# Two-layer attention and FFN block in one kernel: the residual add after each norm moved from VectorE to GpSimd

## The chip, the cores and the metric

One NeuronCore of one Trainium2 chip runs the whole program. The metric is the device time of one execution in microseconds, as the median of three runs. All times below are microseconds unless marked otherwise.

## The reference

Two decoder layers over 256 tokens and 2048 features, everything in float32. Layer 0 has sliding-window attention with sinks, layer 1 a compressed, selected and windowed attention; both have a convolutional feed-forward part with 5632 hidden features. What matters here is how a layer is joined up: each of its two parts works on a normalised copy of `x`, and its result is normalised again before it is added to `x`.

```python
def rmsnorm(x, g):
    xf = x.astype(F32)
    y = xf * lax.rsqrt(jnp.mean(xf * xf, axis=-1, keepdims=True) + RMS_EPS)
    return (y * g.astype(F32)).astype(x.dtype)

def reference(x, norm_g, ...):
    for i in range(DEPTH):
        g = norm_g[i]
        h = rmsnorm(x, g[0])
        ...
        x = x + rmsnorm(mix, g[1])
        h = rmsnorm(x, g[2])
        x = x + rmsnorm(conv_ffn(h, ffn_w_gate[i], ffn_w_up[i], ffn_conv_w[i], ffn_conv_b[i], ffn_w_down[i]), g[3])
    return x
```

## The kernel before

The weights come in as 703 chunks of 128 x 1024 through a ring of four buffers (`raw`). ScalarE copies each chunk to a rounded high part (`whi`, line 1268), VectorE subtracts to get the low part (`wlo`, line 1713, called a split below), and TensorE multiplies high and low parts with the high and low parts of the activations (`hs`). All orders are written out by hand: each engine has one program, and semaphores join them.

`x` lies in SBUF with tokens on the partitions, as `x_sb[128, 8 chunks, 2 token tiles, 256 features]`; `y`, the result of a layer's part, has the same form. `y` is made by units of 512 features (two chunks); the last of them (k = 3) ends in two PSUM banks, one for each token tile, and is multiplied there by the norm's gains (`gain_rows`). The factor r of y's norm is one number per token, `r_token[:, t]`, ready for token tile 0 first (`inverse_of_y`, line 1770).

There are four places where `y` times r is added to `x`. Three of them are followed by the next norm and the next matmuls (called norm A after layer 0's attention, norm B between the layers, norm C after layer 1's attention); the fourth is the end of the program, the tail. In norms A, B and C VectorE runs `norms`: it adds the first 128 features of chunk 0, token tile by token tile (line 1934), then the rest of chunk 0, scales y's last token tile (`last_y`), and then adds the chunks 1 to 7 in between its other work (`add_y`, line 1901): the low parts of the new `hs` (`low_of_h`, line 1787) and the splits of the weights g0+3 to g0+7. TensorE turns each chunk of `x` by four transposes (`turn_x`, line 852) into PSUM, one chunk ahead of the one that it multiplies: before chunk c of the first unit it turns chunk c+1, waits for `h_ready` of chunk c, and then does 16 products and their low parts. ScalarE (`prenorm`) makes the high part of chunk c (`high_of_h`, line 1338), then the weight copy of chunk c+2 of the following ones, then the squares of x for the next norm's sum:

```python
for c in range(CH):
    high_of_h(n, gain, c)
    if 1 <= c <= 5:
        split(g0 + c + RING - 2)
    if 2 <= c <= 5:
        square_x(n, c - 2)
```

`square_x(n, q)` squares the chunks 2q and 2q+1 and waits until they are added. So the squares of the chunks 6 and 7 (q = 3) stand in ScalarE's queue behind chunk 5's high part and ahead of chunk 6's.

In the tail TensorE sums chunks 0 and 1 itself, by products with the identity and with a diagonal of r; VectorE adds the chunks 2 to 7 (lines 1923 and 1901), TensorE turns them, ScalarE copies them to `out_f` (line 1701), and SyncE sends them off in six transfers.

GpSimd works in the attention (lines 640 to 674), copies 128 x 16 coefficients per feed-forward unit (line 691), and makes layer 1's bias tables (lines 552 to 594), which start just when norm B does.

## Time and profile before

| what | value |
|---|---|
| time, median of 3 runs | 2131.49 (2131.29 to 2131.70) |
| span of the profiled execution | 2130.6 |
| TensorE busy | 2115.8 (99%) |
| VectorE, ScalarE, GpSimd busy | 63%, 50%, 12% |
| norm C: last product of the unit before to first product of the next | 1370.46 to 1373.33 |
| tail: last product with weights starts, span ends | 2117.16, 2130.6 |

A row of the timeline gives start, duration, engine, line and operation, and in brackets how long the engine stood idle before it and what ended that. Rows that follow each other are merged with a count (x4), and their duration is then that of all. Durations on GpSimd are rough, so the spacing of its rows counts as much.

### The profile page before, as it was taken

The page shows a single profiled execution, that of the slowest core. Times are in us where ns is not written, and L with a number is a line of the kernel's source. Part 1 is how long each engine was busy: PE and PEld are TensorE (multiplying, and loading weights), DVE is VectorE, ACT ScalarE, POOL GpSimd, SP SyncE. Part 2 cuts the span into 40 slices and gives each one's busy share as a digit, 9 for nine tenths or more (in the row PEclk, how much of TensorE's full clock was granted, in tenths as well). Part 3 has the DMA queues.
Part 4 walks back from the last instruction along what each step waited for, and adds up shares of the span by engine and source line. Part 5 has one row for each costly group of instructions (what it writes and reads, how often), then busy time and mean ns, then how long its engine had stood idle before and what let it go on. Part 6 is the DMA issues. An engine that isn't in the chain of part 4 may idle for free.

```text
span 2130.6 us, 34642 instructions
## 1 busy us (share of the span) xinstructions
PE 2115.8 (99%) x12227; PEld 1811.8 (85%) x12227; DVE 1334.2 (63%) x2031; ACT 1065.4 (50%) x1620; POOL 259.4 (12%) x411
## 2 busy tenths in 40 slices
PE   9999999999999999999999999999999999999998
PEld 8997788888888888888999977888888888888887
DVE  7665676766767754445866654676766767754443
ACT  6675554444444444444656776554444444444443
POOL 4452000000000000002204662000000000000000
PEclk9999999999999999999999999999999999999999
DMA  7444555555555565554673233455555565565553
GB/s 252 144 166 152 175 177 196 180 192 183 179 203 179 189 213 189 188 188 161 222 234 119 100 110 128 166 177 194 182 190 186 178 200 184 187 212 188 188 188 124
DMA packets 107504, 381.42 MB, mean 179 GB/s; under 512 B 14146, under 2 KB 14866, under 8 KB 106770
## 3 DMA queue, kind: packets, MB, share of 16 engines
q1 hardware_dynamic: 105106, 373.63, 52.1%
q10 hardware_dynamic: 2304, 6.53, 0.8%
q8 instruction: 61, 1.00, 0.2%
q14 instruction: 33, 0.27, 0.0%
HBM read 377.97 MB, written 2.14 MB: 178 GB/s over the span
## 4 chain that ended last, share of the span: by engine, by line
PE 96%; DVE 2%; ACT 0%; issue 0%; DMA 0%; SPq 0%; DVEq 0%; ACTq 0%
PE set L708 32%; PE set L801 31%; PE set L712 16%; PE set L926 10%; PE set L1000 2%; PE set L974 1%; PE set L1029 1%; PE set L852 1%; PE set L976 0%; PE set L1031 0%; DVE block_f L2133 0%; DVE wlo L1713 0%; DVE x_sb L1901 0%; DMA raw<-in_stream 0%; PE set L1098 0%
## 5 line engine op out<-in xcount | busy, mean ns | idle before, releaser
L1713 DVE TENSOR_TENSOR wlo<-raw,whi 128x1024 fp32r<-128x1024 f32 x703 | 860.9, 1235 | 578.8 <-ACT whi L1268 575.5
L1268 ACT ACTIVATE whi<-raw 128x1024 fp32r<-128x1024 f32 x703 | 738.2, 1058 | 732.8 <-PE set L712 350.2
L708 PE MATMUL set<-hs,whi 128*128 128x512 f32 x2932 | 966.3, 395 | 0.8 <-ACT whi L1268 0.8
L712 PE MATMUL set<-hs,wlo 128*128 128x256 f32 x2944 | 695.6, 281 | 0.0
L712 PEld LDWEIGHTS set<-hs,wlo 128*128 128x128 f32 x2944 | 544.7, 188 | 61.0 <-DVE wlo L1713 0.4
L708 PEld LDWEIGHTS set<-hs,whi 128*128 128x128 f32 x2932 | 503.3, 189 | 71.0 <-DVE hs L1803 1.0
L801 PE MATMUL set<-whi,hid 128*128 128x512 f32 x1408 | 388.3, 395 | 0.0
L801 PEld LDWEIGHTS set<-whi,hid 128*128 128x128 f32 x1408 | 264.1, 188 | 65.7 <-DVE wlo L1713 0.6
L801 PE MATMUL set<-wlo,hid 128*128 128x512 f32 x704 | 224.1, 395 | 0.0
L926 PE MATMUL set<-hs,whi 128*128 128x256 f32 x1280 | 213.1, 286 | 1.7 <-DVE v_raw L2163 1.4
L926 PEld LDWEIGHTS set<-hs,whi 128*128 128x128 f32 x1280 | 176.2, 189 | 5.0 <-DVE v_raw L2163 1.8
L801 PEld LDWEIGHTS set<-wlo,hid 128*128 128x128 f32 x704 | 132.2, 188 | 31.0
L801 PE MATMUL set<-whi,os 128*128 128x512 f32 x512 | 147.6, 398 | 0.0
L691 POOL COPY cw<-conv_sb 128x16 f32 x20 | 40.8, 2040 | 854.0 <-DVE gate L2272 854.0
L926 PE MATMUL set<-hs,wlo 128*128 128x256 f32 x640 | 131.9, 281 | 0.0
L801 PEld LDWEIGHTS set<-whi,os 128*128 128x128 f32 x512 | 94.5, 188 | 20.1
L1740 DVE TENSOR_TENSOR gate_in<-half,set 128x256 f32<-128x256 f32 x176 | 62.3, 417 | 67.7 <-ACT half L1280 67.7
L926 PEld LDWEIGHTS set<-hs,wlo 128*128 128x128 f32 x640 | 99.9, 188 | 0.0
L1472 ACT ACTIVATE probs<-scored,neg_max 128x128 f32<-128x128 f32 x192 | 85.5, 450 | 14.8 <-DVE neg_max L2007 14.8
L650 POOL TENSOR_SCALAR probs<-probs,recip,gates 128x128 f32<-128x128 f32 (+1 forms) x128 | 84.8, 675 | 66.2 <-DVE recip L2041 66.2
L801 PE MATMUL set<-wlo,os 128*128 128x512 f32 x256 | 89.8, 405 | 0.0
L1280 ACT ACTIVATE half<-set 128x1024 f32<-128x1024 f32 x46 | 47.2, 1026 | 80.7 <-PE set L708 80.7
(209 smaller groups left out, 1339.9 us busy)
## 6 DMA issues: line engine op xcount, KB each, us to landing
raw<-in_stream SPq DMA_DIRECT2D x703, 512.0 KB, 3.4
gain_rows<-rows ACTq DMA_DIRECT2D x4, 1024.0 KB, 4.7
xT<-in_x SPq DMA_DIRECT2D x8, 256.0 KB, 8.2
out_y<-out_f SPq DMA_DIRECT2D x3, 512.0 KB, 3.6
bo_rows<-rows ACTq DMA_DIRECT2D x1, 1024.0 KB, 7.2
wg_raw<-in_w_gates ACTq DMA_DIRECT2D x1, 768.0 KB, 5.1
raw<-in_stream SPq DMA_DIRECT2D x2, 256.0 KB, 3.9
w2k_sb<-in_w ACTq DMA_DIRECT2D x2, 128.0 KB, 8.0
```

Of the source, the lines that this page charges most:

```text
L650: ins = nc.gpsimd.tensor_scalar(e, e, r, gates[:, t, c:c + 1], ALU.mult, ALU.mult)
L691: nc.gpsimd.tensor_copy(cw[:].rearrange("p a b -> p (a b)"), conv_sb[:, layer, f, :]).then_inc(cw_ready, 1)
L708: return mm(sets[set_of(u)][:, t, 0:2 * w], whi[:, slot, cols], r, start=first, stop=final)
L712: return mm(sets[set_of(u)][:, t, w:2 * w], wlo[:, slot, cols], r[:, 0:w], start=False, stop=False)
L801: ins = mm(sets[0][:, CK * (k % 2) + t, :], source[:, kt, part], w[:, g % RING, cols], start=kt == 0 and i == 0, stop=final)
L926: ins = mm(sets[0][:, banks[t // 2], (t % 2) * S:(t % 2 + 1) * S], w, r[:, S:2 * S] if i == 1 else r[:, 0:S], start=kt == 0 and i == 0 and ...
L1000: ins = nc.tensor.transpose(ps_turned[:, t * P:(t + 1) * P], e[:, t * P:(t + 1) * P], ident[:])
L1268: A(whi[:, slot, :], raw[:, slot, :], ACT.Copy).then_inc(hi_ready, 1)
L1280: A(half[:, st, :, 0:width], sets[st][:, :, 0:width], ACT.Copy).then_inc(half_ready, UT)
L1472: ins = A(probs[:, pair_block % 2, b, h, cols], scored[:, b, h, cols], ACT.Exp, bias=neg_max[:, b, h, t:t + 1], scale=-1.0, accum_out=sums ...
L1713: V.tensor_tensor(wlo[:, slot, :], raw[:, slot, :], whi[:, slot, :].bitcast(F32), ALU.subtract).then_inc(lo_ready, 1)
L1740: ins = V.tensor_tensor(dst(t), h, b, ALU.add)
```

## The change

GpSimd gets a new piece of program, `add_residual`. In norms A, B and C it does all of the chunks 1 to 7: for each, two multiplications by r (one for each token tile), a wait for them, and one addition of 128 x 512. Between chunks 1 and 2 it scales y's last token tile by the gains. Since GpSimd can't read PSUM, ScalarE copies that tile from PSUM to `y` first (`copy_last_y`, in norms B and C between the two token tiles of the first high part; after layer 0's attention it lies in SBUF already). VectorE keeps chunk 0, the low parts and the splits. TensorE and the squares wait for the new semaphore `x_more`. In the tail GpSimd adds chunk 4 and then scales the last tile; VectorE adds the chunks 2, 3, 5 and token tile 0 of 6 and 7, waits for `y_last`, adds token tile 1 of 6 and 7, and then copies chunk 7 from PSUM to `out_f` in ScalarE's place. TensorE's own sums in the tail now go chunk by chunk.

```diff
+TAIL_ADDED = ((2, 3, 5, 6, 7), (4,))
...
+            def scale_last_y(n):
+                gain = gain_rows[:, 3 * UNIT:4 * UNIT].rearrange("p (a f) -> p a f", a=CK)
+                part = y[:, 3 * CK:4 * CK, 1, :]
+                pool.wait_ge(rows_in, 16 * (n + 1))
+                pool.wait_ge(y_squared, 8 * n + 8)
+                pool.wait_ge(evacuated, UT * ((O0, DN0, O1, DN1)[n] + 4))
+                nc.gpsimd.tensor_tensor(part, part, gain, ALU.mult).then_inc(y_last, 1)
+                pool.wait_ge(y_last, n + 1)
+
+            def add_residual(n, parts):
+                if n == 0:
+                    pool.wait_ge(y_scaled, 7)
+                else:
+                    pool.wait_ge(evacuated, UT * ((DN0, O1, DN1)[n - 1] + 3) + CK)
+                for k, c in enumerate(parts):
+                    if n < 3 and c == 2:
+                        scale_last_y(n)
+                    for t in range(TT):
+                        pool.wait_ge(y_inverse, TT * n + t + 1)
+                        nc.gpsimd.tensor_scalar(y[:, c, t, :], y[:, c, t, :], r_token[:, t:t + 1], 1.0, ALU.mult,
+                                                ALU.mult).then_inc(y_times_r, 1)
+                    pool.wait_ge(y_times_r, TT * ((CH - 1) * n + k + 1))
+                    nc.gpsimd.tensor_tensor(x_sb[:, c], x_sb[:, c], y[:, c], ALU.add).then_inc(x_more, 1)
+                if n == 3:
+                    scale_last_y(n)
...
@@ turn_x (TensorE)
-                    pe.wait_ge(x_ready, CH * (n - 1) + c + 1 - (TURNED_SUMS if n == 4 else 0))
+                elif n < 4:
+                    pe.wait_ge(x_more, (CH - 1) * (n - 1) + c)
...
@@ square_x (ScalarE)
-                    act.wait_ge(x_ready, CH * (n - 1) + CK * (q + 1))
+                    act.wait_ge(x_ready, n)
+                    act.wait_ge(x_more, (CH - 1) * (n - 1) + CK * q + 1)
...
+            def copy_last_y(n):
+                act.wait_ge(evacuated, UT * ((DN0, O1, DN1)[n - 1] + 3) + CK)
+                A(y[:, 3 * CK:4 * CK, 1, :], sets[0][:, CK + 1, :].rearrange("p (a f) -> p a f", a=CK),
+                  ACT.Copy).then_inc(evacuated, CK)
...
@@ norms (VectorE)
                 add_y(0, 1, x_ready, 1, slice(P, FC))
-                last_y()
                 low_of_h(n + 1, gain, 0)
-                add_y(1, 2, x_ready, 1)
-                add_y(2, 4, x_ready, 2)
                 low_of_h(n + 1, gain, 1)
                 split(g0 + 3)
                 low_of_h(n + 1, gain, 2)
-                add_y(4, 6, x_ready, 2)
                 split(g0 + 4)
                 low_of_h(n + 1, gain, 3)
-                add_y(6, 8, x_ready, 2)
                 split(g0 + 5)
...
@@ tail (VectorE)
-                    for c in range(3, CH):
+                    for c in (3, 5):
                         add_y(c, c + 1, x_ready, 1)
-                        if c == 4:
-                            last_y()
+                    for t in range(TT):
+                        if t == 1:
+                            dve.wait_ge(y_last, n + 1)
+                        for c in (6, 7):
+                            ins = V.scalar_tensor_tensor(x_sb[:, c, t, :], y[:, c, t, :], r_token[:, t:t + 1], x_sb[:, c, t, :],
+                                                         ALU.mult, ALU.add)
+                            if t == 1:
+                                ins.then_inc(x_ready, 1)
+                    dve.wait_ge(x_turned, CH * 5)
+                    for kt in range(CK):
+                        V.tensor_copy(out_f[:, KT - CK + kt, :],
+                                      norm_banks[4][:, (CH - 1) % UT, kt * S:(kt + 1) * S]).then_inc(out_more, 1)
```

VectorE's queue at norm A, before (`hs` is the activations' high and low part, `wlo` a split):

```order
L1770 RECIPROCAL r_token<-root 128x1
L1934 SCALAR_TENSOR_TENSOR x_sb<-y,r_token,x_sb 128x128
L1901 SCALAR_TENSOR_TENSOR x_sb<-y,r_token,x_sb 128x128 x2
L1873 TENSOR_TENSOR y<-y,gain_rows 128x2x256
L1784 SCALAR_TENSOR_TENSOR hs<-set,g_sb,hs 128x128 x2
L1787 SCALAR_TENSOR_TENSOR hs<-set,g_sb,hs 128x256
L1901 SCALAR_TENSOR_TENSOR x_sb<-y,r_token,x_sb 128x256 x2
L1901 SCALAR_TENSOR_TENSOR x_sb<-y,r_token,x_sb 128x2x256 x2
L1787 SCALAR_TENSOR_TENSOR hs<-set,g_sb,hs 128x256 x2
L1713 TENSOR_TENSOR wlo<-raw,whi 128x1024
```

and now:

```order
L1815 RECIPROCAL r_token<-root 128x1
L1982 SCALAR_TENSOR_TENSOR x_sb<-y,r_token,x_sb 128x128
L1946 SCALAR_TENSOR_TENSOR x_sb<-y,r_token,x_sb 128x128 x2
L1829 SCALAR_TENSOR_TENSOR hs<-set,g_sb,hs 128x128 x2
L1832 SCALAR_TENSOR_TENSOR hs<-set,g_sb,hs 128x256 x3
L1758 TENSOR_TENSOR wlo<-raw,whi 128x1024
```

All adds behind chunk 0 and the last scaling are gone from this queue; the low parts and the splits have closed up. GpSimd's queue at the same place, with what its instructions wait for (the copy of `cw` was the next instruction there before, and now stands behind all of these):

```order
L635 TENSOR_SCALAR y<-y,r_token 128x256 [waits y_inverse,y_scaled]
L635 TENSOR_SCALAR y<-y,r_token 128x256 [waits y_inverse]
L638 TENSOR_TENSOR x_sb<-x_sb,y 128x512 [waits y_times_r]
L621 TENSOR_TENSOR y<-y,gain_rows 128x2x256 [waits evacuated,y_squared,rows_in]
L635 TENSOR_SCALAR y<-y,r_token 128x256 [waits y_inverse,y_last]
L635 TENSOR_SCALAR y<-y,r_token 128x256 [waits y_inverse]
L638 TENSOR_TENSOR x_sb<-x_sb,y 128x512 [waits y_times_r]
L635 TENSOR_SCALAR y<-y,r_token 128x256 [waits y_inverse] x2
L638 TENSOR_TENSOR x_sb<-x_sb,y 128x512 [waits y_times_r]
```

The last two rows come for each chunk from 3 to 7. What VectorE did in 8 instructions behind chunk 0's, GpSimd does in 22, one behind the other.

## Rows read from the trace of the kernel before

**Rows 1.** The page: span, busy time of TensorE, the chain that ended last.

```profile
span 2130.6 us, 34642 instructions
...
PE 96%; DVE 2%; ACT 0%; issue 0%; DMA 0%; SPq 0%; DVEq 0%; ACTq 0%
```

**Rows 2.** The timeline of TensorE in norm C and at norm A's start.

```profile
1375.49 0.66 PE L852 MATMUL set<-ident,x_sb 128*128 128x128 f32 x4 [0.44 <-DVE x_sb L1901]
1377.38 0.60 PE L852 MATMUL set<-ident,x_sb 128*128 128x128 f32 x4
1377.99 0.73 PE L708 MATMUL set<-hs,whi 128*128 128x512 f32 x2
...
1390.60 0.60 PE L852 MATMUL set<-ident,x_sb 128*128 128x128 f32 x4
...
1393.83 0.60 PE L852 MATMUL set<-ident,x_sb 128*128 128x128 f32 x4
1394.18 0.72 PE L708 MATMUL set<-hs,whi 128*128 128x512 f32 x2
...
252.82 0.33 PE L852 MATMUL set<-ident,x_sb 128*128 128x128 f32 x1 [1.49 <-DVE x_sb L1934]
```

**Rows 3.** The timeline of VectorE and ScalarE in norm C.

```profile
1371.93 0.16 DVE L1770 RECIPROCAL r_token<-root 128x1 f32<-128x1 f32 x1 [0.28 <-ACT root L1428]
...
1372.40 0.61 DVE L1901 SCALAR_TENSOR_TENSOR x_sb<-y,r_token,x_sb 128x128 f32<-128x128 f32 x2
...
1383.19 1.41 DVE L1901 SCALAR_TENSOR_TENSOR x_sb<-y,r_token,x_sb 128x512 f32<-128x512 f32 x2
...
1389.68 0.62 ACT L1323 ACTIVATE unread<-x_sb 128x512 f32<-128x512 f32 x1
...
1390.82 0.19 ACT L1323 ACTIVATION_READ_ACCUMULATOR unread<-x_sb 128x1 f32 x1
...
1391.24 0.84 ACT L1338 ACTIVATE hs<-set,g_sb 128x256 fp32r<-128x256 f32 x2 [0.23 <-PE set L852]
...
1392.11 0.88 DVE L1787 SCALAR_TENSOR_TENSOR hs<-set,g_sb,hs 128x256 fp32r<-128x256 f32 x2 [0.91 <-ACT hs L1338]
```

**Rows 4.** GpSimd's instructions by line: ns minimum/median/maximum of one.

```profile
L640 POOL TENSOR_TENSOR probs<-probs x32: 453/462/471, 68.1 to 180.2; 128x128 f32<-128x128 f32 x32
L641 POOL TENSOR_SCALAR probs<-probs,recip x32: 364/374/1347, 68.5 to 180.6; 128x128 f32<-128x128 f32 x32
L604 POOL TENSOR_TENSOR vc_g<-vc_rep,own_head x8: 1037/1044/2042, 1126.9 to 1275.0; 128x512 fp32r<-128x512 f32 x8
```

**Rows 5.** A group of GpSimd's instructions by form: busy us, mean ns, idle before.

```profile
L540 POOL TENSOR_TENSOR fold<-ident 128x64 f32<-128x64 f32 x1 | 0.3, 320 | 0.1
```

**Rows 6.** GpSimd beside VectorE in norm B, timeline.

```profile
999.49 0.52 POOL L570 TENSOR_SCALAR bias<-dist 128x384 f32<-128x384 f32 x1
...
1000.15 0.40 POOL L552 TENSOR_SCALAR_AFFINE_SELECT bias<-bias 128x128 f32<-128x128 f32 x1
...
1012.71 1.41 DVE L1713 TENSOR_TENSOR wlo<-raw,whi 128x1024 fp32r<-128x1024 f32 x1
...
1013.13 1.37 POOL L570 TENSOR_SCALAR bias<-dist 128x384 f32<-128x384 f32 x1
```

**Rows 7.** The tail, timeline of VectorE and ScalarE.

```profile
2118.63 0.17 DVE L1770 RECIPROCAL r_token<-root 128x1 f32<-128x1 f32 x1
...
2119.04 0.48 DVE L1923 SCALAR_TENSOR_TENSOR x_sb<-y,r_token,x_sb 128x256 f32<-128x256 f32 x1
2119.43 1.67 DVE L1901 SCALAR_TENSOR_TENSOR x_sb<-y,r_token,x_sb 128x256 f32<-128x256 f32 x4
...
2121.74 2.46 DVE L1901 SCALAR_TENSOR_TENSOR x_sb<-y,r_token,x_sb 128x256 f32<-128x256 f32 x6
...
2124.95 0.66 ACT L1701 ACTIVATE out_f<-set 128x256 f32<-128x256 f32 x2 [0.19 <-PE set L852]
```

**Rows 8.** A stretch around norm A's idle time: busy per engine, granted clock.

```profile
252.00:253.00 1.00, 0.18 (x2) 0.19 (x3) 0.90 (x5) 0.69 (x3) 0.00 (x0) 1.00 0.92 377
```

More of the change, by code:

```diff
@@ L84 @@
 FIRST_PRODUCTS = 10
-OUT_PARTS = [(0, 4, 2), (4, 8, 4), (8, 12, 6), (12, 14, 7), (14, 15, 8), (15, 16, 9)]
+TAIL_ADDED = ((2, 3, 5, 6, 7), (4,))
+OUT_PARTS = [(0, 4, 2, 0), (4, 8, 4, 0), (8, 12, 6, 0), (12, 14, 7, 0), (14, 15, 7, 1), (15, 16, 7, 2)]
 def first_chunk(u):
@@ L351, in build_program @@
         x_half, x_half_turned, h_hi_half, h_half = sem("x_half"), sem("x_half_turned"), sem("h_hi_half"), sem("h_half")
+        x_more, y_last, y_times_r, out_more = sem("x_more"), sem("y_last"), sem("y_times_r"), sem("out_more")
         x_ready, x_turned, h_hi_ready, h_ready = sem("x_ready"), sem("x_turned"), sem("h_hi_ready"), sem("h_ready")
@@ L524, in _ @@
             fetch_run(first_chunk(O1 + 2), CHUNKS)
-            for lo, hi, copies in OUT_PARTS:
-                sp.wait_ge(out_ready, copies)
+            for lo, hi, by_scalar, by_vector in OUT_PARTS:
+                sp.wait_ge(out_ready, by_scalar)
+                if by_vector:
+                    sp.wait_ge(out_more, by_vector)
                 sp.dma_start(out[:, lo:hi], out_f[:, lo:hi]).then_inc(out_done, 16)
@@ L684, in _ @@
                     mask_turned(PAIRS[0] - 1)
+                add_residual(2 * layer, range(1, CH))
                 ff = FF0 if layer == 0 else FF1
@@ L692, in _ @@
                                           conv_sb[:, layer, f, :]).then_inc(cw_ready, 1)
+                add_residual(2 * layer + 1, range(1, CH) if layer == 0 else TAIL_ADDED[1])
         @block.tensor
@@ L831, in turn_x @@
                     pe.wait_ge(x_half, TT * (n - 1) + 1)
+                elif n < 4:
+                    pe.wait_ge(x_more, (CH - 1) * (n - 1) + c)
+                elif c in TAIL_ADDED[0]:
+                    pe.wait_ge(x_ready, n + TAIL_ADDED[0].index(c))
                 else:
-                    pe.wait_ge(x_ready, CH * (n - 1) + c + 1 - (TURNED_SUMS if n == 4 else 0))
+                    pe.wait_ge(x_more, (CH - 1) * (n - 1) + TAIL_ADDED[1].index(c) + 1)
                 if n == 4 and c >= UT:
@@ L844, in turn_x @@
                                 ins.then_inc(x_half_turned, 1)
-                                pe.wait_ge(x_ready, CH * (n - 1) + 1)
+                                pe.wait_ge(x_ready, n)
                         if n == 0:
@@ L1245, in _ @@
                     mm(o, x_sb[:, c, t, f], ident[:], start=n == 0, stop=False)
-            for half_of in range(TT):
-                pe.wait_ge(diag_part, half_of + 1)
-                for c in range(TURNED_SUMS):
+            for c in range(TURNED_SUMS):
+                for half_of in range(TT):
+                    pe.wait_ge(diag_part, half_of + 1)
                     for n, (t, f, o) in enumerate(tail_tiles(c)):
@@ L1334, in high_of_h @@
                             ins = A(hs[:, 0, t * P:(t + 1) * P], src, ACT.Copy, scale=g_sb[:, gain, 0:1])
+                            if t == 0 and n > 1:
+                                copy_last_y(n - 1)
                         ins.then_inc(h_hi_half, 1)
@@ L1697, in _ @@
                     unit(dn + k, y_evac(dn + k, n + 1, k), norm_next=k == 3)
-            for c in range(CH):
+            copy_last_y(3)
+            for c in range(CH - 1):
                 act.wait_ge(x_turned, CH * 4 + c + 1)
-                for part in [slice(0, CK)] if c < CH - 1 else [slice(0, 1), slice(1, 2)]:
-                    A(out_f[:, c * CK + part.start:c * CK + part.stop, :],
-                      norm_banks[4][:, c % UT, part.start * S:part.stop * S].rearrange("p (a s) -> p a s", s=S),
-                      ACT.Copy).then_inc(out_ready, 1)
+                A(out_f[:, c * CK:(c + 1) * CK, :], norm_banks[4][:, c % UT, :].rearrange("p (a s) -> p a s", s=S),
+                  ACT.Copy).then_inc(out_ready, 1)
         @block.vector
```

9 lines of the change are left out of this document (1 added, 8 removed).

## The prediction

> **What bounds the kernel now.** I read the page first. TensorE is on 96% of the chain that ended last, VectorE on 2% [rows 1]. So the change can win only what TensorE idles at the three norms and in the tail, and it loses whatever it makes TensorE wait. I then read TensorE's timeline in norm C, which stands for A and B as well, and noted each row with idle time in front of it. Once the norm's products have begun there is one such row on `x`: the turning of chunk 1 waits 0.44 for VectorE's add (1375.49). Afterwards the turning of a chunk comes every 3.23 us (1390.60 to 1393.83), with 2.8 us of products between, and TensorE never stops; chunk 6's products start at 1394.18 [rows 2]. From here on I count in us after 1370: turn 1 at 5.49, turn 2 at 7.38, turn 7 at 23.83, products of chunk 6 at 24.18.
>
> VectorE's and ScalarE's timeline shows the slack. VectorE has added chunks 6 and 7 by 14.60 (1383.19 plus 1.41). ScalarE squares them from 19.68 to 21.01, makes chunk 6's high part from 21.24, VectorE its low part from 22.11 to 22.99, and TensorE needs it at 24.18 [rows 2, 3]. The squares thus have their data 5 us early, and the high part has 1.2 us to spare.
>
> **What the change removes.** In each norm the wait of 0.44 before turn 1 can go, if GpSimd is quicker with chunk 1. VectorE is relieved of seven chunks' adds at 0.70 each (half of 1.41 [rows 3]), but it is not late anywhere behind that, so this brings nothing. Of the tail see below.
>
> **What it adds: one serial chain on GpSimd.** Prices first. A multiplication by r has 128 x 256 elements; a 128 x 128 one of that kind takes 0.374 [rows 4], a plain 128 x 384 one 0.52 [rows 6]. I take 0.45, so 0.90 for two. Behind a completion GpSimd's next instruction starts about 0.15 later (999.49 + 0.52 = 1000.01, next at 1000.15) [rows 6]. The addition has 128 x 512 elements and two inputs. The trace has two relatives: the 128 x 512 product of line 604 with 1.04, whose inputs are broadcast, and the 128 x 128 sum of plain inputs with 0.462 [rows 4]. With the plain 128 x 64 sum at 0.320 [rows 5] the plain form costs 2.2 ns a column, which gives 0.462 + 384 x 0.0022 = 1.31. I take 1.2, nearer to the plain form, and keep 1.04 and 1.31. A chunk is then 0.90 + 0.15 + 1.2 = 2.25, against 0.70 on VectorE.
>
> To that comes that the two engines get in each other's way. A GpSimd instruction of 0.52 takes 1.37 when it meets a split, 0.85 more, and the split itself takes 1.41 [rows 6]. I charge 0.9 for each split that GpSimd meets, with 0.8 and 1.07 as the ends (my estimates: 0.85 less a little, and three quarters of 1.41). There is one split per chunk of TensorE's work, so a chunk costs GpSimd 3.15, against TensorE's 3.23: it keeps pace, and gains nothing.
>
> Chain in norm C. r of token tile 1 is there at 2.09, VectorE's adds of chunk 0 run until 3.01 [rows 3]; the two engines mix there, and chunk 1's addition starts at about 3.2. It ends at 4.4, early enough: turn 1 comes at about 5.1 instead of 5.49, and since chunk 0's adds will be up to 0.35 later for the same mixing, the gain is 0.1 to 0.4. Then the scaling of the last tile, 4.4 to 5.6; 0.15; two multiplications to 6.65; 0.15; the addition to 8.0. TensorE turns chunk 2 at 8.1 instead of 7.38, and products start at about 8.5 instead of 7.99: **0.5 lost**. Five more chunks (3 to 7) at 2.25 and five splits at 0.9 give 8.1 + 11.25 + 4.5 = 23.85 for chunk 7. TensorE would turn it at 8.1 + 5 x 3.23 = 24.3, so it is not late for that.
>
> But it is late for the squares. They stand in ScalarE's queue ahead of chunk 6's high part and now wait for GpSimd's last chunk. Squares 23.9 to 25.2 (1.33), high part from 25.2, low part starts 0.87 later and takes 0.88: 27.0 [rows 3]. Products of chunk 6 start at 27.0 instead of 24.18: **2.8 lost per norm**, the 0.5 included. Behind that chunk 7 has a whole chunk's products as cover, and the weights are four chunks ahead, so no further stall follows. The squares q = 2 (waiting for chunk 5, at about 17.6) delay chunk 5's high part too, but end at 19.0, and its low part is ready at 20.8, where TensorE needs it at 21.5: hidden, by 0.7.
>
> Bounds of this term: with additions at 1.04 the eight 128 x 512 operations give 1.3 less, splits at 0.8 another 0.5, multiplications at 0.374 another 1.0; then chunk 7 comes at 21.1, the squares fit in, and only 0.3 from chunk 2 is left. With 1.31 and 1.07 it is 0.9 + 0.85 more, so 4.5. Norms A and B have the same instructions (A without ScalarE's copy of 0.6, which ends beside TensorE's turning of token tile 1 anyway and may cost up to 0.1; in B the bias tables used to disturb VectorE and now come later, a gain that I put at nothing). Three norms: 3 x 2.8 = **8.4**, between 0.9 and 13.5.
>
> **The tail.** Today VectorE's last add ends at 2124.20 (2121.74 plus 2.46), and ScalarE's last copy ends at 2125.61 [rows 7]. Now VectorE has six adds of 0.42 (1.67 over 4) behind 2119.5 (2.5), then waits for `y_last`, then two more (0.84). GpSimd has behind r of tile 1 (2118.80) one multiplication, a wait, the addition, and the scaling: 0.45 + 0.15 + 1.2 + 1.2 = 3.0. If GpSimd gets in only after VectorE's six, `y_last` comes at 2125.1 and the last add ends at 2126.0, 1.8 late. If they alternate and each GpSimd instruction costs VectorE some two thirds of its duration (1.9 in all), VectorE's six end at 2123.9 and the last add at about 2124.8, 0.6 late; if they don't disturb each other at all, at 2123.2. I take **1.2**, with -0.9 and 1.9 as ends. The last copy moves to VectorE at about the same price (0.66 today), and TensorE's other order of sums hides behind the adds.
>
> **Sum.** 8.4 + 1.2 = 9.6 on the span of 2130.6, so 2140.2. The median of the runs is 0.9 above the span: 2141.1. I say 2141.
>
> **A rule against the trace.** The trace puts GpSimd's chunk at 2.25 against VectorE's 0.70, a factor of 3, since the change also splits one instruction into multiplication and addition. The Trainium skill (GPSIMD Engine Reference, 4.1 Engine selection) says to keep elementwise work on VectorE, GpSimd being about 2x slower with two inputs. By that factor alone a chunk would be 1.4, GpSimd would stay ahead of TensorE even with the splits, and the time would be that of the first rival. No run so far has this addition.
>
> **Rivals.**
> *GpSimd keeps ahead.* If chunk 7 is added by about 21.8, the squares cost nothing. What decides is the chain per chunk with its split: under 2.75 instead of 3.15. [...] Then 0.3 per norm and 0.6 to 1.2 in the tail: +1.5 to +2.5, 2133 to 2134. Chance 0.19.
> *Faster.* The wait of 0.44 goes in three norms and GpSimd is never late, also not with chunk 2 (added by 7.0 instead of 8.1, which needs a 128 x 512 operation under 0.85); TensorE also loses the 0.2 that it waits for chunk 1's low part. With a tail that gains 0.9 that is 3 x 0.6 + 0.9 = 2.7: 2128.8. No row of GpSimd is that quick at this size [rows 4]. Chance 0.03.
> *GpSimd starves.* If VectorE's instructions always go first and each split costs GpSimd 1.41 and more, a chunk takes 3.7, TensorE waits 0.45 at each turning from 3 to 7, and the squares come on top: some 5.5 per norm, 2131.5 + 16.5 + 1.9 = 2150. Chance 0.05.
> *The clock falls.* A stall of 2 to 3 us before chunk 6 is longer than any today. The longest, 1.49 in norm A, left the granted clock at 1.00 [rows 2, 8]. If it fell to 1.2 GHz for one chunk of 2.8 us, each norm would cost 2.8 more: 2149.5. The Trainium skill (TensorE: Matmul & The Clock Gate, Part 1) has idle time as what brings the lower level; by that it could come here, by the row it does not at half the length. Chance 0.05.
> The forecast itself has 0.68.
>
> **How the numbers follow.** What a measurement here can tell from no change is about 0.2%, 4.3 us, so slower begins at 2135.8. The forecast lies above that but for its lower edge (0.03 of its 0.68), the starved and the throttled case lie above it wholly: 0.65 + 0.05 + 0.05 = 0.75. Within: 0.03 + 0.19 and a third of the fast rival's 0.03, whose full gain of 2.7 is inside the bound: 0.23. Faster by more, if chunk 2's gain and the tail's are larger than I worked out: 0.02. The range leaves out the two cases at 2149 and 2150 and the fast one, and takes in the first rival and most of the bounds of the sum (2131.5 + 0.9 to 2131.5 + 15.4): 2133 to 2147.
>
> **What the new profile would show.** GpSimd's 128 x 512 additions at 1.2 and its chunks 3.1 apart in the norms, 1.3 longer where a split meets them. A wait of 0.5 to 0.7 before turn 2. ScalarE idle before the squares q = 3, released by GpSimd, and TensorE idle for about 2.3 before chunk 6's products, released by VectorE's low part. The splits longer than 1.23. In the tail VectorE idle before token tile 1 of chunk 6, released by GpSimd. The prediction fails if chunk 7 is added before 21.8: then there is no wait at the squares, and the norms cost next to nothing.

## The result and the profile after

The changed kernel takes 2141.52 (median of 5 runs, 2140.45 to 2142.13), the kernel before 2131.29 beside it (2130.90 to 2131.70). The ratio is 1.0047, with an interval of 1.0037 to 1.0058: **slower by 10**. The profiled execution took 2141.52, with a span of 2139.7.

The page of the changed kernel first, answering to [rows 1]: span, busy times, the chain that ended last.

```profile
span 2139.7 us, 34696 instructions
...
PE 2118.8 (99%) x12227; PEld 1814.6 (85%) x12227; DVE 1327.7 (62%) x2003; ACT 1064.7 (50%) x1621; POOL 332.3 (16%) x481
...
PE 95%; DVE 2%; POOL 1%; issue 1%; ACT 1%; DMA 0%; DVEq 0%; ACTq 0%; POOLq 0%
```

GpSimd, which was not in the chain at all, now has 1% of it. Its new instructions by line in the changed kernel (multiplications by r, additions, the scaling), where rows 4 and 5 had only relatives:

```profile
L635 POOL TENSOR_SCALAR y<-y,r_token 128x256 f32<-128x256 f32 x44 | 33.1, 763 | 734.8 <-DVE r_token L1815 734.5
L638 POOL TENSOR_TENSOR x_sb<-x_sb,y 128x512 f32<-128x512 f32 x22 | 30.1, 1368 | 1.8
...
L621 POOL TENSOR_TENSOR y<-y,gain_rows 128x512 f32<-128x512 f32 x4 | 5.4, 1360 | 0.0
```

The means include the waiting for VectorE. What one costs undisturbed stands in the timeline of norm C. To lay kernels on each other I count in each norm from the start of VectorE's reciprocal for token tile 0 ("after r": 1371.11 before, 1377.91 now). TensorE's timeline of norm C, changed kernel, the rows that answer to [rows 2]:

```profile
1381.19 0.44 PE L890 MATMUL set<-ident,x_sb 128*128 128x128 f32 x2 [1.51 <-DVE x_sb L1946]
...
1382.89 0.60 PE L890 MATMUL set<-ident,x_sb 128*128 128x128 f32 x4
...
1384.74 0.66 PE L890 MATMUL set<-ident,x_sb 128*128 128x128 f32 x4
...
1401.20 0.60 PE L890 MATMUL set<-ident,x_sb 128*128 128x128 f32 x4
...
1404.00 0.73 PE L742 MATMUL set<-hs,whi 128*128 128x512 f32 x2 [2.21 <-DVE hs L1832]
```

Two waits: 1.51 for VectorE's last add of chunk 0, which the prediction did not have, and 2.21 before chunk 6's products, which it had (2.3). Turn 1 comes 4.98 after r (4.38 before), turn 2 6.83 (6.27), turn 7 23.29 (22.72), chunk 6's products 26.09 (23.07): **3.02 lost**, of which 0.57 stand from the start on.

The same stretch on GpSimd, VectorE and ScalarE, answering to [rows 3] (the row that begins with L1946 gives the two adds of 1379.21 one by one, as ns minimum/median/maximum):

```profile
1379.21 1.92 DVE L1946 SCALAR_TENSOR_TENSOR x_sb<-y,r_token,x_sb 128x128 f32<-128x128 f32 x2
...
L1946 DVE SCALAR_TENSOR_TENSOR x_sb<-y,r_token,x_sb x2: 571/1001/1431, 1379.2 to 1379.7; 128x128 f32<-128x128 f32 x2
...
1379.72 1.26 POOL L638 TENSOR_TENSOR x_sb<-x_sb,y 128x512 f32<-128x512 f32 x1
1380.94 1.33 POOL L621 TENSOR_TENSOR y<-y,gain_rows 128x512 f32<-128x512 f32 x1
...
1384.67 0.93 POOL L635 TENSOR_SCALAR y<-y,r_token 128x256 f32<-128x256 f32 x2
...
1393.07 1.30 POOL L638 TENSOR_TENSOR x_sb<-x_sb,y 128x512 f32<-128x512 f32 x1
...
1393.94 1.51 DVE L1758 TENSOR_TENSOR wlo<-raw,whi 128x1024 fp32r<-128x1024 f32 x1
...
1394.34 1.91 POOL L635 TENSOR_SCALAR y<-y,r_token 128x256 f32<-128x256 f32 x2
...
1396.34 1.30 POOL L638 TENSOR_TENSOR x_sb<-x_sb,y 128x512 f32<-128x512 f32 x1
...
1399.61 1.29 POOL L638 TENSOR_TENSOR x_sb<-x_sb,y 128x512 f32<-128x512 f32 x1
...
1400.98 0.63 ACT L1361 ACTIVATE unread<-x_sb 128x512 f32<-128x512 f32 x1 [3.52 <-issue]
...
1402.22 0.82 ACT L1384 ACTIVATE hs<-set,g_sb 128x256 fp32r<-128x256 f32 x2
...
1403.07 0.88 DVE L1832 SCALAR_TENSOR_TENSOR hs<-set,g_sb,hs 128x256 fp32r<-128x256 f32 x2 [0.56 <-ACT hs L1384]
```

Read from below: the low part that TensorE waits for follows the high part, that follows the squares, and those begin 0.08 after GpSimd's last addition ends (1399.61 + 1.29 = 1400.90), with ScalarE idle for 3.52. The view names no releaser for that idle time ("issue"), but the instants leave only `x_more`. Above: GpSimd's addition of chunk 1 starts just as VectorE's last add of chunk 0 does (1379.72, the add at 1379.7), that add takes 1.43 instead of about 0.35, and the pair 1.92 instead of 0.61. In between: a split that starts 0.43 before GpSimd's addition ends takes 1.51 instead of 1.23, and the two multiplications that start before that split ends take 1.91 instead of 0.93. Chunks come every 3.27.

Norms A and B have something that norm C has not. Windows of the changed kernel, with the granted clock after the busy times (then DMA's share and GB/s), at norm A's start (answering to [rows 8]), behind norm B's wait, and at norm C's:

```profile
253.00:255.00 2.00, 0.73 (x4) 0.69 (x4) 1.78 (x3) 0.37 (x1) 2.00 (x2) 0.60 0.00 0
255.00:257.00 2.00, 2.00 (x11) 2.00 (x11) 0.48 (x1) 0.47 (x1) 1.82 (x4) 0.50 0.00 0
257.00:259.00 2.00, 2.00 (x9) 1.87 (x9) 0.00 (x0) 0.55 (x2) 1.92 (x4) 0.50 0.04 8
...
1028.00:1030.00 2.00, 2.00 (x9) 1.67 (x8) 2.00 (x3) 0.66 (x1) 1.40 (x3) 0.56 0.01 4
1030.00:1032.00 2.00, 2.00 (x9) 1.76 (x8) 0.75 (x1) 0.78 (x1) 1.77 (x3) 0.59 0.69 240
...
1400.00:1404.00 4.00, 1.79 (x12) 1.39 (x10) 1.09 (x4) 3.02 (x10) 1.04 (x2) 1.00 0.35 127
1404.00:1408.00 4.00, 4.00 (x22) 3.51 (x23) 3.56 (x7) 2.69 (x3) 0.00 (x0) 1.00 0.12 24
```

In norm A the clock falls to 1.2 GHz at about 253.4, within the second of the two waits at the start (1.50, and 1.27 until 254.31); in norm B it falls behind the wait before chunk 6 (2.26); in norm C the same wait (2.21) leaves it at 1.00.

The tail of the changed kernel, answering to [rows 7]:

```profile
2129.45 1.31 POOL L638 TENSOR_TENSOR x_sb<-x_sb,y 128x512 f32<-128x512 f32 x1
2129.56 3.68 DVE L1946 SCALAR_TENSOR_TENSOR x_sb<-y,r_token,x_sb 128x256 f32<-128x256 f32 x4
...
2130.73 1.44 POOL L621 TENSOR_TENSOR y<-y,gain_rows 128x512 f32<-128x512 f32 x1
...
2133.17 1.66 DVE L1970 SCALAR_TENSOR_TENSOR x_sb<-y,r_token,x_sb 128x256 f32<-128x256 f32 x4
...
2135.62 0.75 DVE L1976 COPY out_f<-set 128x256 f32<-128x256 f32 x2 [0.79 <-PE set L890]
```

Four adds take 3.68 instead of 1.67 while GpSimd adds and scales (2.75), and nothing waits for `y_last`: the scaling is done at 2132.17, VectorE comes to it at about 2134.0. The last copy ends 8.84 after r instead of 7.90.

So the ledger, by the distances from r to r (before: A to B 746.42, B to C 372.48, C to tail 746.60; now 749.38, 377.21, 749.62): norm A +2.96, B +4.73, C +3.02, tail +0.94, together 11.65. Two small pieces go the other way: norm A's r comes 0.89 earlier, and the profiled execution ends 5.15 behind the last copy, against about 5.9. Neither belongs to the change: r of norm A comes at 251.1 to 251.8 in all the kernels below too, whatever they change behind it, and the last piece lies between 5.0 and 6.9 in them. 2131.49 + 11.65 - 0.89 - 0.7 = 2141.5. The ledger is that of one execution: its mean granted clock is 0.997, that of the four others 0.999, and they took 2140.45 to 2142.13, so the falls in the ledger needn't be in them.

### The profile page after: what moved, and what is told of

Same layout as the page of the kernel before. It is cut to its first block, busy times and chain, and to the rows that moved or that the text cites. A ratio compares the mean times of both kernels' runs of the same rounds, so it can differ in the third digit from the quotient of the medians.

```text
span 2139.7 us, 34696 instructions
## 1 busy us (share of the span) xinstructions
PE 2118.8 (99%) x12227; PEld 1814.6 (85%) x12227; DVE 1327.7 (62%) x2003; ACT 1064.7 (50%) x1621; POOL 332.3 (16%) x481
## 4 chain that ended last, share of the span: by engine, by line
PE 95%; DVE 2%; POOL 1%; issue 1%; ACT 1%; DMA 0%; DVEq 0%; ACTq 0%; POOLq 0%
PE set L835 31%; PE set L742 31%; PE set L746 16%; PE set L964 10%; PE set L1038 1%; PE set L1012 1%; PE set L1067 1%; POOL y L635 1%; POOL x_sb L638 1%; PE set L1014 0%; PE set L1069 0%; DVE block_f L2176 0%; DVE wlo L1758 0%; PE set L890 0%; ACT whi L1305 0%
## 5 line engine op out<-in xcount | busy, mean ns | idle before, releaser
L635 POOL TENSOR_SCALAR y<-y,r_token 128x256 f32<-128x256 f32 x44 | 33.1, 763 | 734.8 <-DVE r_token L1815 734.5
```

What stands on the lines that cost most here:

```text
L635: nc.gpsimd.tensor_scalar(y[:, c, t, :], y[:, c, t, :], r_token[:, t:t + 1], 1.0, ALU.mult, ALU.mult).then_inc(y_times_r, 1)
```

## The experiments

Times are medians of 5 to 11 runs each; the kernel before had 2131.5, 2131.4 and 2131.7 beside them. The table takes up the profiled execution of each: what each norm costs against the distances of before, and an f where the granted clock fell in that norm.

| kernel | time | norm A | norm B | norm C | tail | wait before chunk 6 (C) |
|---|---|---|---|---|---|---|
| changed kernel | 2141.52 | 2.96 f | 4.73 f | 3.02 | 0.94 | 2.21 |
| old tail | 2140.55 | 4.40 f | 3.39 | 3.00 | 0.00 | 2.24 |
| TensorE kept busy | 2139.75 | 2.98 | 3.34 | 3.01 | 0.96 | 0.67 |
| squares later | 2134.81 | 1.96 f | 1.11 | 0.73 | 0.96 | none |
| VectorE adds 6 and 7 | 2135.61 | 1.25 | 1.24 | 1.24 | 0.95 | none |
| GpSimd starts later | 2145.34 | 5.03 f | 5.33 f | 5.05 f | 0.96 | 2.39 |
| both mends | 2135.50 | 1.30 | 1.69 | 1.31 | 0.95 | none |
| both mends, old tail | 2134.88 | 1.28 | 1.60 | 1.29 | 0.00 | none |
| the same, scaling later | 2137.03 | 1.20 f | 3.71 f | 3.12 f | 0.00 | none |
| VectorE keeps chunk 1 | 2136.05 | 1.44 f | 1.72 | 1.35 | -0.01 | none |
| GpSimd adds 4 to 7 only, late | 2131.93 | -0.02 | 0.91 | -0.26 | 0.00 | none |

### Squares later

The theory is that what TensorE waits for before chunk 6 is not the chunk but the squares in ScalarE's queue. The rival is that GpSimd's pace alone makes it late.

```diff
@@ prenorm (ScalarE), behind high_of_h(n, gain, c)
-                    if 2 <= c <= 5:
+                    if 2 <= c <= 4:
                         square_x(n, c - 2)
+                    if c == 6:
+                        square_x(n, 3)
@@ norms (VectorE): low_of_h(..., 6) ahead of the sum of the squares
-                token_sum(sq_x, x_squared, 8 * (n + 2))
                 low_of_h(n + 1, gain, 6)
+                token_sum(sq_x, x_squared, 8 * (n + 2))
```

> The changed kernel, but the squares of chunks 6 and 7 stand behind chunk 6's high part on ScalarE, and the sum of squares behind chunk 6's low part on VectorE. Theory 1: the stall of 2.2 to 2.3 before chunk 6 goes in norms B and C, and with it B's fall of the clock; left are 0.6 from the late turn 2 and 0.3 at chunk 7, whose low part now waits for the sum. Norm A, where the clock falls after two stalls at the start, stays at about +3. 3 + 0.9 + 0.9 + 0.9 for the tail is 5.7: 2137. Rival (VectorE's splits, slowed from 1.23 to 1.5 by GpSimd, hold up the low parts whatever the order): 2141.5, no change.

Measured 2134.81 (2133.56 to 2136.21), ratio 1.0017 (1.0008 to 1.0026). ScalarE's timeline in norm C of this kernel:

```profile
1393.81 0.84 ACT L1384 ACTIVATE hs<-set,g_sb 128x256 fp32r<-128x256 f32 x2 [1.14 <-PE set L890]
...
1396.20 0.63 ACT L1361 ACTIVATE unread<-x_sb 128x512 f32<-128x512 f32 x1 [1.55 <-issue]
```

The squares still wait for GpSimd's last addition (it ends at 22.98 after r, as in the changed kernel, 22.99), but the high part is now ahead of them, and no wait before chunk 6 is left in any norm. 6.7 of the 10.2 are gone: the order in the queue was the larger part of the loss. It is 2.3 in norm C, 3.6 in B with the fall of the clock behind the wait, and 1.0 in A, where the changed kernel had no such wait. It came out 2 below what was expected: A costs 1.96 where 3 was expected, C 0.73, and the clock fell in A alone, at the start.

### VectorE adds chunks 6 and 7

The same question from the other side: shorten GpSimd's chain instead of moving its reader. VectorE adds 6 and 7 behind chunk 3's low part, ahead of its third split of the norm.

```diff
+PER = 5
@@ GpSimd
-                add_residual(2 * layer, range(1, CH))
+                add_residual(2 * layer, range(1, PER + 1))
@@ norms (VectorE)
                 low_of_h(n + 1, gain, 3)
+                dve.wait_ge(y_last, n + 1)
+                add_y(6, 8, x_ready, 2)
```

> The changed kernel, but VectorE adds chunks 6 and 7 in the norms, where it did before (behind chunk 3's low part), and GpSimd only 1 to 5. The order of the squares is as in the changed kernel. Theory 1: the squares q = 3 no longer wait for GpSimd's last chunks, so the stall before chunk 6 goes as with the moved squares; the stall at the start and the late turn 2 stay: 0.6 per norm and 1 to 2 more in A if its clock falls, 0.9 in the tail: 2134 to 2136. Rival (it is ScalarE's order itself that costs, whoever adds): 2141.5.

Measured 2135.61 (2134.17 to 2138.19), ratio 1.0021 (1.0012 to 1.0030). The squares start at 20.40 in norm C, and no wait is left before chunk 6. In its place stands a new one before turn 5 in TensorE's timeline:

```profile
1390.18 0.66 PE L893 MATMUL set<-ident,x_sb 128*128 128x128 f32 x4 [0.52 <-POOL x_sb L639]
```

VectorE's two adds and the split behind them held up GpSimd's multiplications for chunk 5, which took 2.86 there instead of 1.91. GpSimd has no slack: what it meets beyond one split per chunk puts it behind TensorE.

### GpSimd starts chunk 1 later

Theory: the wait of 1.5 at the start arises because GpSimd's first addition gets in between VectorE's adds of chunk 0. GpSimd now waits until VectorE is through with these.

```diff
                     pool.wait_ge(y_times_r, TT * ((CH - 1) * n + k + 1))
+                    if n < 3 and c == 1:
+                        pool.wait_ge(x_ready, n + 1)
```

> The changed kernel, but in norms A, B and C GpSimd's first addition (chunk 1) waits until VectorE has added chunk 0, so it can't slip in between VectorE's last two adds (1.92 us for the two instead of 0.61 in the changed kernel's trace, TensorE idle 1.3 to 1.5 before it turns the rest of chunk 0). Theory 1 (GpSimd's serial chain is what costs, through the squares in ScalarE's queue): the stall at the start goes, but GpSimd begins 0.3 later, so turn 2 and the squares come 0.3 later: 0 to 0.3 more per norm, 2141.5 to 2142.5; norm A keeps its clock and gets the stall before chunk 6 instead. Rival (the late adds of chunk 0 are what costs): 1.3 less per norm, 2137.5.

Measured 2145.34 (2142.66 to 2148.05), ratio 1.0061 (1.0047 to 1.0074): **slower**, which neither expectation had. Its timeline of TensorE in norm C:

```profile
1382.87 0.44 PE L892 MATMUL set<-ident,x_sb 128*128 128x128 f32 x2 [0.42 <-DVE x_sb L1948]
...
1387.93 0.66 PE L892 MATMUL set<-ident,x_sb 128*128 128x128 f32 x4 [1.38 <-POOL x_sb L640]
...
1407.29 0.73 PE L744 MATMUL set<-hs,whi 128*128 128x512 f32 x2 [2.39 <-DVE hs L1834]
```

The mechanism at the start is right: the pair of adds takes 0.83, and the wait falls from 1.51 to 0.42. But GpSimd's chain now starts 0.47 later (2.28 after r against 1.81), and TensorE gets the time back as a wait of 1.38 before turn 2 (7.24 after r, 6.83 in the changed kernel). The whole chain stays late (turn 7 at 23.59 against 23.29), and the wait before chunk 6 is 2.39. Norm A kept its clock at the start, as expected, but behind the wait before chunk 6 the clock fell in all three norms of this execution; without that (26.60 against 23.07) the norm would cost 3.5, 0.5 more than in the changed kernel. The five executions lie from 2142.66 to 2148.05, and the one whose mean granted clock is 1.000 took 2142.78, next to the 2142.5 that the theory had as its upper end. That points at the clock for the rest of the loss, but doesn't show it: one execution at 0.998 took 2142.66.

### Both mends, and both with the old tail

> The first two edits together. Theory 1: no stall long enough for the clock to fall in any norm, 0.9 to 1.2 left in each (turn 2, chunk 7's low part) and 0.9 in the tail: 2131.3 + 3 to 4.5, about 2135. Rival (start): 2137.5 as with the first edit alone. Rival (splits): 2141.5.

Measured 2135.50 (2134.57 to 2138.10), ratio 1.0020 (1.0011 to 1.0029), as expected. With the squares out of the way what is left per norm is 1.3: turn 2 waits 1.39 for GpSimd, and TensorE runs at GpSimd's pace of 3.27 afterwards (turn 7 at 23.63, 0.9 late); the last 0.4 come behind that, at chunk 7's first products, where the expectation of *Squares later* had 0.3 for a low part that now waits for the sum of the squares. With the old tail as well:

> The changed kernel with both mends of the norms (GpSimd begins chunk 1 only when VectorE is through with chunk 0; the squares of chunks 6 and 7 stand behind chunk 6's high part) and the old tail. Theory (effects add up): 2135.5 of both mends less 0.95 of the tail, so 2134.5; left is about 1 in each norm, the wait before turn 2 on GpSimd's second chunk. Rival (the tail's price was not its own): 2135.5 again.

Measured 2134.88 (2134.45 to 2135.99), ratio 1.0016 (1.0007 to 1.0025); the tail is back at 7.90. The step of 0.6 between the medians is less than the scatter of either, so the tail's price rests on the traces, where it is 0.95 in each pair.

### The old tail alone

Only the tail's part of the change is undone: VectorE adds the chunks 2 to 7 and scales, ScalarE does the last copies, TensorE sums in the old order.

```diff
-TAIL_ADDED = ((2, 3, 5, 6, 7), (4,))
+TAIL_ADDED = ((2, 3, 4, 5, 6, 7), ())
@@ GpSimd
-                if n == 3:
-                    scale_last_y(n)
...
-                add_residual(2 * layer + 1, range(1, CH) if layer == 0 else TAIL_ADDED[1])
+                if layer == 0:
+                    add_residual(1, range(1, CH))
```

> The changed kernel with the tail of before (VectorE adds chunks 2 to 7 and scales the last tile, ScalarE copies chunk 7, TensorE's sums in the old order). Theory 1: the tail's share of the loss is 0.9 (from r of token tile 0 to the last copy's end: 7.90 before, 8.84 after), so 2140.6. Rival: what follows the last copy took 5.0 before and 3.3 after in the profiled executions, so if that is real and not chance, the new tail is 0.7 faster and this run gives 2142.2.

Measured 2140.55 (2139.67 to 2142.51), 0.97 below the changed kernel, which is less than the scatter; the tail's 7.90 in the trace is that of before. In this execution the clock fell in norm A behind a wait of 2.19 before chunk 6, and not in B and C behind 2.24 each.

### TensorE kept busy in the waits

Does the clock's fall follow from the waits? Here products of a matrix of ones with the identity, into a part of PSUM that is written over later and that nobody reads, fill most of the two waits: 4 at the start, 7 before chunk 6. They can't take a wait away.

```diff
@@ turn_x, ahead of the wait for chunk 0's remaining features
+                                for _ in range(4):
+                                    mm(sets[1][:, UT - 1, 0:P], ones[:], ident[:], start=True, stop=True)
@@ ahead of the wait for h_ready of chunk 6
+                    if n > 0 and c == 6:
+                        for _ in range(7):
+                            mm(norm_banks[n][:, UT - 1, 0:P], ones[:], ident[:], start=True, stop=True)
```

> The changed kernel with products whose result nobody reads in TensorE's two waits of each norm: four before the rest of chunk 0 is turned, seven between the turning of chunk 7 and chunk 6's products. Theory 2 (part of the loss is TensorE's clock, which falls to 1.2 GHz behind one of the two waits in some of the norms: a fall behind the squares' wait costs 1.4 or so, 4.4 instead of 3.0 from r to r): granted clock 1.00 throughout, each norm 3.0 slower than before, one to two falls fewer than in the changed kernel: 2139 to 2140. Rival (the falls cost nothing, since the clock is back before the next wait, as in the changed kernel's norm A, where the squares' wait vanished behind the fall): 2141.5.

Measured 2139.75 (2139.65 to 2141.13), ratio 1.0043 (1.0029 to 1.0057). The waits left are 0.62 and 0.67, and the granted clock is 1.00 in all norms (the mean of each of the five executions is 1.000). The changed kernel's median is 1.8 higher, but its runs (2140.45 to 2142.13) overlap with these, so the price of a fall is read from the traces. Its windows at norm A's start:

```profile
254.00:256.00 2.00, 1.94 (x17) 1.94 (x18) 1.01 (x4) 0.47 (x1) 1.90 (x3) 1.00 0.00 0
256.00:258.00 2.00, 2.00 (x16) 1.78 (x14) 0.73 (x2) 1.60 (x3) 1.92 (x4) 1.00 0.03 8
```

Norm B goes from 4.73 to 3.34, norm A stays (2.98 against 2.96). Slow products at norm A's start gave GpSimd time to catch up: the wait before chunk 6 was absent there in the changed kernel, and it is back (0.63, with the dummy products ahead of it). So a fall at the start is paid by the wait behind it, where there is one; with the squares moved there is none, and norm A costs 1.96 with its fall, against 0.73 in norm C. A fall before chunk 6 is paid in full, 1.4.

### Scaling later

Both mends and the old tail; in addition GpSimd scales y's last tile between chunks 2 and 3 instead of between 1 and 2, to be in time with turn 2.

```diff
-                    if n < 3 and c == 2:
+                    if n < 3 and c == 3:
                         scale_last_y(n)
```

> Both edits (first addition waits for chunk 0, squares behind chunk 6's high part), the tail of before, and GpSimd scales y's last tile behind chunk 2 instead of ahead of it. Theory 1: chunk 2 is then added 1.3 sooner, at 5.9 after r instead of 7.2, and turn 2 (6.0 to 6.3) doesn't wait; chunk 3 comes at about 9.7 against a turning at 9.5, and GpSimd's pace of 3.27 per chunk against TensorE's 3.24 loses 0.1 to 0.2 more: 0.2 to 0.5 per norm, 0 in the tail: 2132 to 2133. Rival (what is left of the loss is the two engines in each other's way, wherever the scaling stands): 2134.6, the two edits' 2135.5 less the tail's 0.9.

Measured 2137.03 (2134.47 to 2138.39), ratio 1.0026 (1.0014 to 1.0037): **a miss**. From norm C's timelines, GpSimd and TensorE:

```profile
1382.43 1.79 POOL L635 TENSOR_SCALAR y<-y,r_token 128x256 f32<-128x256 f32 x2
1384.30 2.15 POOL L640 TENSOR_TENSOR x_sb<-x_sb,y 128x512 f32<-128x512 f32 x1
...
1386.51 0.87 PE L891 MATMUL set<-ident,x_sb 128*128 128x128 f32 x4 [1.91 <-POOL x_sb L640]
```

Turn 2 is in time (5.92 after r; in the kernel before 6.27). But now GpSimd meets two splits in a row with chunk 3, one in the multiplications and one in the addition (1.79 and 2.15 instead of 0.93 and 1.29), and turn 3 waits 1.91 until 11.29. Behind that the clock fell in norms B and C of this execution (B 3.71, C 3.12). The two of the seven executions with a mean granted clock of 1.000 took 2134.47 and 2134.66, about the 2134.88 of the kernel without this edit: what turn 2 gains turn 3 loses, and the falls seem to be the rest. The expectation worked out the serial chain and charged one split per chunk, as in the prediction; the first two splits stand close together.

### VectorE keeps chunk 1

The changed kernel with the old tail, but VectorE adds chunk 1, and GpSimd starts at chunk 2 (this addition waits for VectorE's chunk 0), with the scaling ahead of chunk 3; the squares stand in the changed kernel's order.

```diff
@@ GpSimd
-                add_residual(2 * layer, range(1, CH))
+                add_residual(2 * layer, range(2, CH))
@@ norms (VectorE), behind chunk 0's low part
+                add_y(1, 2, x_ready, 1)
```

> The changed kernel with the tail of before; in the norms VectorE keeps chunk 1 as well, GpSimd's first addition is chunk 2 and waits for VectorE's chunk 0, and the last tile is scaled behind it. Squares in the changed kernel's order. Theory 1: GpSimd is one chunk (2.3) ahead, its last chunk comes 20 to 20.8 after r instead of 23, within what the squares have to spare, so nothing waits but turn 1 (0.4 as before, up to 0.9 if GpSimd's scaling is in the way of VectorE's add): 2131.3 to 2133. Rival (any chain on GpSimd costs through the slower splits): 2135 and more.

Measured 2136.05 (2134.27 to 2136.62), ratio 1.0020 (1.0011 to 1.0029): the squares are in time, as expected, the time is **not**. From norm C's timelines, GpSimd, VectorE and TensorE:

```profile
1376.77 1.26 POOL L621 TENSOR_TENSOR y<-y,gain_rows 128x512 f32<-128x512 f32 x1
...
1376.81 2.12 DVE L1951 SCALAR_TENSOR_TENSOR x_sb<-y,r_token,x_sb 128x256 f32<-128x256 f32 x2
...
1378.99 0.66 PE L893 MATMUL set<-ident,x_sb 128*128 128x128 f32 x4 [1.71 <-DVE x_sb L1951]
```

VectorE's two adds of chunk 1 start 0.04 behind a 128 x 512 operation of GpSimd and take 2.12, against 0.88 in the kernel before. Turn 1 comes at 5.75 instead of 4.38, and the norm costs 1.35, about that delay. The clock fell in norm A of this execution, at about 253.5, and there TensorE's one long wait until then is the one that the kernel before has too. TensorE's first row behind it, and the window with the fall:

```profile
251.78 0.33 PE L893 MATMUL set<-ident,x_sb 128*128 128x128 f32 x1 [1.50 <-DVE x_sb L1978]
...
253.00:255.00 2.00, 1.93 (x10) 1.85 (x11) 1.57 (x5) 0.77 (x2) 1.83 (x2) 0.61 0.01 4
```

GpSimd hurts also where it is nobody's source, by standing in VectorE's way while VectorE is.

### GpSimd adds chunks 4 to 7 only, and late

This is the kernel before with GpSimd's part reduced to where it should cost nothing: VectorE adds 0 to 3 and scales, GpSimd starts when chunk 3 is done.

```diff
+            def add_residual(n):
+                pool.wait_ge(x_ready, 4 * n + 4)
+                for k, c in enumerate(range(4, CH)):
...
@@ norms (VectorE)
-                add_y(4, 6, x_ready, 2)
...
-                add_y(6, 8, x_ready, 2)
```

> The kernel before, but GpSimd adds chunks 4 to 7 (the same two multiplications and one addition for each, nothing else), starting only when VectorE has added chunk 3; VectorE keeps chunks 0 to 3 and the scaling of y's last token tile, ScalarE's squares wait for the same chunks as ever, the tail is that of before. Theory (GpSimd's adds cost nothing where they begin behind VectorE's adds of chunks 0 to 3 and end before the squares ask for them): GpSimd starts about 5.7 after r, has chunk 4 at about 9 (TensorE turns it at about 12.9) and chunk 7 at about 18.5 to 19 (the squares ask at 19.0 to 19.7 in norm C), no wait on GpSimd before any turn; time 2131.4, +-0.7, gaps from norm to norm as before (746.4, 372.5, 746.6). Rival (GpSimd beside VectorE costs something wherever it stands, through longer splits and low parts): 0.5 to 1 per norm, 2133 to 2134.5. If chunk 7 comes only at 21, the squares are up to 1 late: 2132 to 2133.

Measured 2131.93 (2130.98 to 2132.86) against 2131.67, ratio 1.0002 (0.9993 to 1.0011): **no difference**. GpSimd and ScalarE in norm C:

```profile
1377.41 1.29 POOL L619 TENSOR_TENSOR x_sb<-x_sb,y 128x512 f32<-128x512 f32 x1
...
1388.23 1.29 POOL L619 TENSOR_TENSOR x_sb<-x_sb,y 128x512 f32<-128x512 f32 x1
...
1389.61 0.63 ACT L1341 ACTIVATE unread<-x_sb 128x512 f32<-128x512 f32 x1 [0.28 <-issue]
```

The last addition ends 18.62 after r, the squares begin at 18.71 (18.57 before), and TensorE waits for GpSimd nowhere. GpSimd's chunks there are as slow as ever (3.6 on average, 1377.41 to 1388.23 over three). They cost nothing since each is added 3.9 to 5.0 ahead of its turn. They bring nothing either, VectorE having been late nowhere but at turn 1, which it still adds. Not as expected is norm B, 0.91 over its distance of before (see *Left open*). No kernel of this study is faster than the one before.

## Why the prediction was right, point by point

**The mechanism in the norms: right, and shown.** The serial chain keeps pace with TensorE, the last chunk is late for the squares, and these hold up chunk 6's high part. Moving the squares or shortening the chain leaves no such wait in any norm, and GpSimd's work is the same in the first of the two. Forecast were 2.8 per norm; without a fall of the clock it is 3.0 (norms A and C with TensorE kept busy, and norm C as it is), 3.3 in B.

**The prices.** The addition takes 1.26 to 1.30 undisturbed, predicted 1.2 with 1.31 as the upper end: the plain form's 2.2 ns a column was the right guide, and line 604's 1.04 was not. The multiplications take 0.93 for two (0.90). A split met costs 0.98 (1.91 less 0.93; predicted 0.9). The pace is 3.27 (3.15), and chunk 7 is added 22.99 after r; the forecast 23.85 after 1370 is 22.74 after r. So the last chunk came out 0.25 off, and chunk 6's products 0.2 (26.09 against 25.89).

**The start: the term was mis-sized.** The prediction let chunk 0's adds come "up to 0.35 later" and booked a gain of 0.1 to 0.4 at turn 1. They come 1.31 later (1.92 against 0.61), one whole addition of GpSimd, and turn 1 is 0.60 late. Turn 2 is 0.56 late, near the prediction (0.7, and 0.5 at the products), but for another cause: GpSimd had chunk 2 ready just in time (6.77 after r, turn 2 at 6.83), and the delay came down from chunk 0. The wait of 0.5 to 0.7 before turn 2 that the new profile was to show isn't there. The run that starts GpSimd later shows the forecast's cause behind the other: it waits 1.38 for GpSimd at turn 2 instead.

**The clock: a rival that came true in part.** The prediction gave the fall 0.05 and 2.8 a norm, from one row of 1.49 at 1.00 [rows 8]. In the changed kernel's profiled execution it fell in two of three norms, at 1.4 in norm B and at nothing net in norm A. What share of the median's 10 the falls have is less sure: it is 1.8 by the 2139.75 of the kernel that keeps TensorE busy, with runs that overlap. The one row was also no proof that such a wait is harmless: its window ends 0.18 behind the wait, and the same wait of 1.49 to 1.50 had a fall behind it in norm A of two later kernels (scaling later, VectorE keeps chunk 1). That the single number came out so near, 2141.0 against 2141.5, is partly chance: the norms cost 10.7 instead of 8.4 (9.3 with the clock held), and 1.6 go back by the two pieces that the change doesn't touch. The Trainium skill (TensorE: Matmul & The Clock Gate, Part 1) names idle time as what brings the lower level; the windows agree so far that each fall here has a wait ahead of it. What decides whether a given wait does it stays open: 2.24 left the clock alone twice with the old tail, and 2.19 in that same execution did not.

**The tail.** Predicted 1.2, measured 0.94. The case "they alternate" was the right one (VectorE's four adds lose 2.0 of their own, 1.9 assumed for six), but nothing waits for `y_last`, and VectorE's last four adds run undisturbed. A slip in the sum changes nothing: without disturbance the last add would end at 2122.8, not at 2123.2.

**The rivals.** *GpSimd keeps ahead* fell with the pace of 3.27 against the 2.75 that it needed. *Starves* fell too: GpSimd is held up once per chunk, for less than a split. *Faster* needed an addition under 0.85. The Trainium skill's factor of about 2 (GPSIMD Engine Reference, 4.1 Engine selection) fits the addition alone (1.29 against 0.70 for the chunk on VectorE, 1.8). It doesn't fit the chunk, which is 3.2 times 0.70 before any split, since the fused instruction became three.

**Left open.** Norm B costs some 0.35 more than A and C in most kernels, and 0.9 in the last one, where its turns are not late. The traces say where: in the last kernel TensorE is 0.3 ahead of the kernel before until 44 us after norm B's r, and 0.7 behind it at 52. GpSimd builds layer 1's bias tables there, some 20 later than before, and VectorE's instructions beside them are longer. VectorE in the kernel before, where GpSimd does nothing in this stretch; then VectorE and GpSimd in the last kernel, at the same place:

```profile
1041.83 1.23 DVE L1713 TENSOR_TENSOR wlo<-raw,whi 128x1024 fp32r<-128x1024 f32 x1 [0.89 <-ACT whi L1268]
...
1040.81 1.51 DVE L1731 TENSOR_TENSOR wlo<-raw,whi 128x1024 fp32r<-128x1024 f32 x1 [0.86 <-ACT whi L1284]
...
1040.78 0.51 POOL L582 TENSOR_SCALAR_AFFINE_SELECT bias_c<-bias_c 128x256 f32<-128x256 f32 x1
```

The prediction put the later tables at a small gain that it counted as nothing. No run isolates them. A kernel that runs one GpSimd addition with no reader beside the kernel before, to price the collision alone, wasn't tried.

## What to carry to other kernels

When work moves from a fast engine to a slow one, look beyond the first reader: in this kernel the one that asks earliest for the last piece decided. Look through the queues of the other engines for a side job (here squares for a later sum) that waits for that piece ahead of something urgent, and move it behind. And count the collisions where the fast engine is itself the source: start the slow one only when the fast one is through with what is urgent, and give it only what has a chunk or more of slack; here it then cost nothing, and it brought nothing either, since TensorE was the bound and not VectorE. One profiled execution at the full clock doesn't show that a wait is safe for the clock.

## What the runs showed of the hardware

- VectorE and GpSimd hold each other up by about whole instructions. A 128 x 512 addition of GpSimd (1.26) delays the second of two back-to-back adds of VectorE by about its whole length (the pair takes 1.92 instead of 0.61); two multiplications that start 1.1 before a split ends wait for that end (0.93 to 1.91). The Trainium skill (SBUF — State Buffer, Who interferes with whom) says that a VectorE instruction with two inputs in SBUF contends with a GpSimd instruction that reads SBUF, and that one side has the shared ports for the whole instruction while the other blocks. These rows agree. Which side goes first they don't show: the add that is held up has the earlier start on record (1379.70 against 1379.72). The prediction had charged 0.35.
- They don't strictly alternate. 18 of the 20 copies of `cw` on line 724 in the changed kernel (128 x 16) take about 2.15, the length of two back-to-back splits of VectorE that they lie beside (340.15 to 342.30, the splits from 339.89 to 342.24).
- The granted clock fell to 1.2 GHz behind waits of 1.9 to 2.4, at norm A's start with two waits of 1.50 and 1.27 and 1.1 of products between them, and in two kernels at norm A's start with the 1.49 or 1.50 alone. It also stayed at 1.00 behind waits as long: behind 2.21 to 2.24 in other norms, and behind the 1.49 in the kernel before.
- Four small products in the wait of 1.5 and seven in the one of 2.2 were enough to hold the clock at 1.00 in all three norms, in each of five executions.
